# Attention denominators of a hybrid backbone step: inverted on ScalarE through logarithm and exponential instead of on VectorE

## What is computed

```python
s = jnp.einsum("bkgqd,bkld->bkgql", qblk, k).astype(jnp.float32) * scale
p = jax.nn.softmax(s, axis=-1).astype(v.dtype)
return jnp.einsum("bkgql,bkld->bkgqd", p, v)
```

## Time and profile before

| | |
|---|---|
| median of 3 runs | 1596.38 us (1594.84 to 1597.21) |
| the profiled execution, its own time | 1597.8 us |
| span of its profile | 1596.0 us |
| PE busy | 1369.9 us, 86% of the span |
| DVE busy | 757.0 us, 47% |
| ACT busy | 534.1 us, 33% |

### The profile page before, as it was taken

One profiled execution on the slowest core, in us unless ns is written; L12 is line 12 of the kernel. 1 busy time (PEld: TensorE's weight loads), 2 busy tenths in 40 slices (PEclk: granted clock), 3 DMA queues, 4 the chain that ended last, 5 costly groups with the idle time before them and its releaser, 6 DMA issues.

```text
span 1596.0 us, 32023 instructions
## 1 busy us (share of the span) xinstructions
PE 1369.9 (86%) x13967; PEld 1248.3 (78%) x13967; DVE 757.0 (47%) x1076; ACT 534.1 (33%) x800; POOL 52.8 (3%) x85
## 2 busy tenths in 40 slices
PE   5799999857994599966799778969999999989994
PEld 2799999824552279953699678969999999989993
DVE  3644111065654754546655455256544555434445
ACT  3633222161222423235333422045343343333332
POOL 0000000010000100000100010000000000000000
PEclk8799999957997679985899988989999999999996
DMA  8223232100003500025000064202122221022221
GB/s 373 95 104 112 79 120 94 49 10 1 0 0 151 208 3 7 4 68 224 2 7 4 21 227 159 89 27 80 55 76 79 79 74 57 13 63 76 68 71 66
DMA packets 24605, 123.51 MB, mean 77 GB/s; under 512 B 2912, under 2 KB 3552, under 8 KB 16448
## 3 DMA queue, kind: packets, MB, share of 16 engines
q1 hardware_dynamic: 19888, 100.64, 17.8%
q0 software_dynamic: 4624, 21.47, 3.6%
HBM read 107.22 MB, written 14.88 MB: 77 GB/s over the span
## 4 chain that ended last, share of the span: by engine, by line
PE 75%; DVE 13%; ACT 4%; DMA 4%; issue 2%; PEld 1%; POOL 0%; SPq 0%; POOLq 0%; PEldq 0%; DVEq 0%; ACTq 0%
PE ps L602 41%; PE ps L998 10%; PE ps L845 3%; PE ps L833 3%; PE ps L737 2%; PE ps L813 2%; DVE rden L1438 2%; PE ps L696 2%; PE ps L825 1%; DMA xT<-in_x 1%; PE ps L625 1%; DVE nmax L1421 1%; PE ps L591 1%; PEld ps L625 1%; DMA uc<-u_scratch 1%
## 5 line engine op out<-in xcount | busy, mean ns | idle before, releaser
L1305 DVE TENSOR_TENSOR wlo<-raw,whi 128x2048 fp32r<-128x2048 f32 x48 | 109.7, 2288 | 115.3 <-ACT whi L1047 115.2
L602 PE MATMUL ps<-h2lo,whi 128*128 128x322 f32 x672 | 154.5, 311 | 0.7 <-ACT facc L1085 0.7
L602 PE MATMUL ps<-h2hi,wlo 128*128 128x322 f32 x672 | 155.0, 312 | 0.0
L602 PE MATMUL ps<-h2hi,whi 128*128 128x322 f32 x672 | 154.0, 310 | 0.0
L602 PE MATMUL ps<-hlo,whi 128*128 128x322 f32 x544 | 125.1, 311 | 1.7 <-ACT cacc L1085 1.7
L602 PE MATMUL ps<-hhi,wlo 128*128 128x322 f32 x544 | 125.5, 312 | 0.0
L602 PE MATMUL ps<-hhi,whi 128*128 128x322 f32 x544 | 124.7, 310 | 0.0
L602 PEld LDWEIGHTS ps<-h2hi,whi 128*128 128x128 f32 x672 | 114.2, 190 | 0.0
L602 PEld LDWEIGHTS ps<-h2lo,whi 128*128 128x128 f32 x672 | 113.0, 189 | 0.9 <-issue 0.9
L602 PEld LDWEIGHTS ps<-h2hi,wlo 128*128 128x128 f32 x672 | 113.7, 189 | 0.0
L1047 ACT ACTIVATE whi<-raw 128x2048 fp32r<-128x2048 f32 x48 | 91.8, 1915 | 58.9 <-PE ps L602 48.8
(11 more groups left out here) (291 smaller groups left out, 2751.8 us busy)
## 6 DMA issues: line engine op xcount, KB each, us to landing
raw<-in_wblk SPq DMA_DIRECT2D x48, 1024.0 KB, 4.9
adl<-in_wada SPq DMA_DIRECT2D x8, 2048.0 KB, 11.0
raw<-in_wdn SPq DMA_DIRECT2D x44, 256.0 KB, 2.6
adaw<-in_wada SPq DMA_DIRECT2D x4, 2048.0 KB, 17.1
gate_scratch<-gout POOLq DMA_DIRECT2D x16, 322.0 KB, 2.5
gld<-gate_scratch POOLq DMA_DIRECT2D x8, 644.0 KB, 4.3
u_scratch<-uout POOLq DMA_DIRECT2D x12, 320.0 KB, 2.4
uc<-u_scratch SPq DMA_DIRECT2D x4, 960.0 KB, 6.5
```

The source lines that it names most:

```text
L602: mm = pe.matmul(o, w, v, start=first, stop=last and w is hi and x is xh[n])
L1305: TT(wlo[s][:, :], raw[s][:, :], whi[s][:, :].bitcast(F32), ALU.subtract).then_inc(lo_done, 1)
```

## The change

DVE no longer inverts. ACT computes ln of the denominators out of PSUM into `rden`, and then exp(-x) in place, which is the same reciprocal. DVE only waits for `rden` and multiplies. For heads 0 to 6 the two activations stand in ACT's stream behind the first exponential of the next head (before c = 1); for head 7 and the two context groups they stand behind the last exponential of the phase.

```diff
+        def denominators(h):
+
+            p = h % 2
+            dens = slice(64 - 64 * p, 128 - 64 * p)
+            ac.wait_ge(o_done, h + 1)
+            if h >= 2:
+                ac.wait_ge(o_copied, h - 1)
+            ac.activation(rden[p][dens, :], bank(4 + p)[dens], ACT.Ln).then_inc(lden_done, 1)
+            ac.wait_ge(lden_done, h + 1)
+            ac.activation(rden[p][dens, :], rden[p][dens, :], ACT.Exp, scale=-1.0).then_inc(rden_done, 1)
+
         for h in range(8):
             for c in range(6):
                 m = 6 * h + c
+                if h and c == 1:
+                    denominators(h - 1)
                 ac.wait_ge(st_done, m + 1)
...
             ac.activation(pt[p][:, 0, :], bank(2 + p), ACT.Exp).then_inc(exp_done, 1)
+        for h in range(7, 10):
+            denominators(h)
         phase_over(ac, 3)
...
         def head_out(h):
             p = h % 2
             rows, dens = slice(64 * p, 64 * p + 64), slice(64 - 64 * p, 128 - 64 * p)
-            dv.wait_ge(o_done, h + 1)
-            dv.reciprocal(rden[p][dens, :], bank(4 + p)[dens]).then_inc(rden_done, 1)
             dv.wait_ge(rden_done, h + 1)
```

More of the change, by code:

```diff
@@ L377, in build @@
     qst_done, row_s_done, max_done, diag_done = sem("qk_parts"), sem("row_scores"), sem("score_max"), sem("max_on_diagonal")
+    lden_done = sem("denominators_logged")
     st_done, exp_done, o_done, rden_done, o_copied = (
```

## The result

The change made the kernel slower: 1602.87 us against 1596.47 us (medians of 13 runs each), a ratio of 1.0035 with a 95% interval of 1.0024 to 1.0046. The ratio makes 5.6 us (3.8 to 7.3); the two medians themselves lie 6.4 us apart. The prediction had 1600.3 us in a range of 1597.4 to 1603.4 us.

The account below looks back on a forecast made before the run. The attention was taken as bound by PE waiting at R2 for DVE's reciprocal chain in heads 1 to 6. Terms -0.7 + 1.8 + 2.8 = +3.9 us on 1596.38 gave 1600.3 us, range 1597.4 to 1603.4.

Parts of the forecast that it names:

- The price of a group: On ACT, load, logarithm, load and exponential for one head's denominators: 3.87 us, against 3.35 us for DVE's reciprocal.
- B: ACT's time for one load, logarithm, load and exponential: 3.87 us, with bounds 3.77 and 4.03.
- Heads 1 to 6: PE's 1.80 us stall at R2 becomes 1.69 us ahead of K3; six heads gain 0.7 us.
- Head 7: ACT's four instructions stand before the exponential of K1, delaying K3, which had no stall: 1.8 us lost.
- The end: After the last context exponential, three inversions queue on ACT, so DVE's last multiplication comes 2.8 us later.
- The three places: Attention heads 1 to 6, head 7 and the phase's end: -0.7, +1.8 and +2.8 us.
- the sum: Total over the attention phase: -0.7 + 1.8 + 2.8 = +3.9 us, close to 10 B - 34.8.
- a dearer group: On ACT, the 0.16 us gap between load and logarithm counted to the load: B 4.03 us, total +5.5 us.
- The loads that count for nothing: Rival: ACT's logarithm and exponential served without table switching, about 1.3 us per head, 1580.7 us; chance 0.04.
- The drain around each load: Rival: ACT's pipeline drains at each table switch, making B 6.5 us, total +30, 1626 us; chance 0.03.
- The granted clock: Rival: PE falls to 1.2 GHz in one head, doubling 12.2 us of work: +12, 1612 us; chance 0.03.
- The partly hidden group: Rival: ACT's loads overlap draining work or PE restarts faster; B near 3.5 us, 0 to +1, 1597 us; chance 0.06.

Follow-up runs that it names:

- the runs with the parts alone: Change for heads 0 to 6 only (1598.47 us), and for head 7 and context groups only (1599.83 us), beside 1597.04 before; attention phase grew 1.4 and 2.8 us.

## Why the prediction was right

*The price of a group.* B was put at 3.87 us; the rows of after give 390.82 to 394.66, 3.84 us. Load 1.283, logarithm 0.592 and exponential 0.628 us came out as taken from the norms.

*Heads 1 to 6.* Expected -0.7 us. The last matmul of K0 moves from 390.70 to 389.79 in head 1 and from 474.73 to 473.23 in head 7, so the six heads take 83.44 us instead of 84.03: -0.6 us. The stall changed its releaser from DVE to ACT and kept its size, as the working said. The heads alternate between waits of 1.52 and 1.38 us, since the exponential behind the group overlaps it only in every second head; I had assumed the overlap in all.

*Head 7.* Expected +1.8 us; K3 stands 480.21 - 473.23 = 6.98 us behind K0, against 5.09: +1.9 us.

*The end.* Expected +2.8 us; from the end of the last context exponential to the end of DVE 502.39 - 490.14 = 12.25 us against 9.52: +2.7 us. The multiplication was expected to end near 503.2 us and ended at 502.39, because head 1 itself began 0.9 us earlier in this profile. The three places make 4.0 us, where the sum had 3.9, and the runs with the parts alone gave 1.4 and 2.8 us.

*What stays over.* The ratio says 5.6 us, its interval 3.8 to 7.3. The sum lies at the lower edge. The stretch behind the phase differs by 1.5 us between the two profiles of before and by 2.6 us over all twelve profiles; whether the remaining 1.6 us are this spread or something small and systematic outside the phase is open. No experiment isolates it. So the mechanism and the size of the three places are confirmed, but that 1602.87 us lies inside the range, 0.5 us from its end, owes something to luck: the upper end was made from a dearer group (B = 4.03) and the runs' spread, not from anything outside the phase.

*The rivals.* The loads that count for nothing: false as compiled, but its number, 1580.7 us, is what the kernel without the loads took (1581.37). The drain around each load: no gap above 0.02 us in the chain, and 0.4 us ahead of all twenty loads. The granted clock: it stayed at 1.00 in the heads of the changed kernel's profiles, with waits up to 1.61 us, so the reason to leave it out held. One step further, in the profile with waits of 2.03 us, the clock did fall, but at 1.6 us a head and not at the 12 us that this rival charged for a whole head. The partly hidden group: B was 3.84, not 3.5.

## What to carry to other kernels

Price an activation by what stands around it in its engine's stream: here two table loads cost twice as much as the work they served, and one explicit load of a set holding both functions turned a loss of 5.6 us into a gain of 16.4. Work moved to an engine that is idle on average still delays what is queued behind it; ask which instruction stands there and who waits for it. And look first whether the stall is a matter of place: two halves of the same reciprocal in DVE's own gaps won 11 us with no change of engine.

## What was not expected

In the profiles the cost of ACT's time was not linear. Waits of 1.38 to 1.90 us left the granted clock at 1.00 in these heads; after the four waits of 2.03 to 2.12 us it fell to 1.2 GHz for some 3.4 us each, and one more exponential, 0.5 us per group, cost 11.6 us in the phase of that execution instead of 5.3. Whether the length of the wait alone decides it, these runs do not say.

Second, half a reciprocal took 1.76 us and a whole one 3.35 us, so that cutting it costs only 0.17 us:

```profile
392.15 1.76 DVE L1438 RECIPROCAL rden<-ps 64x256 f32<-64x256 f32 x1
```
